# Four phase boundaries: who makes the shifted columns and one slab's low part, and where the second tile is turned

## The reference

```
for i in range(DEPTH):                                  # first block, DEPTH = 2
    mod_l = split(silu_c @ ada_w[i] + ada_b[i], 6)
    h_l = rmsnorm(x, mix_norm_g[i]) * (1 + mod_l[1]) + mod_l[0]
    y_l = mixer(h_l) if i == 0 else conformer_conv(h_l)
    x = x + mod_l[2] * y_l
    h = rmsnorm(x, ffn_norm_g[i]) * (1 + mod_l[4]) + mod_l[3]
    x = x + mod_l[5] * ((silu(h @ w1) * (h @ w3)) @ w2)
x = rmsnorm(x, final_g)
for l in range(DEPTH):                                  # second block
    x = x + 0.5 * swiglu(rms_norm(x), ffn1_w_in[l], ffn1_w_out[l])
    x = x + mixer(rms_norm(x) @ w_mix_in[l]) @ w_mix_out[l]
    x = x + 0.5 * swiglu(rms_norm(x), ffn2_w_in[l], ffn2_w_out[l])
```

## Time and profile before

| | |
|---|---|
| median of three runs | 1772.92 us |
| the profiled execution, first to last instruction (span) | 1771.1 us |
| TensorE busy | 1696.4 us (96%) |
| VectorE busy | 1104.2 us (62%) |
| ScalarE busy | 807.9 us (46%) |
| GpSimd busy | 48.2 us (3%) |
| low parts of slabs on VectorE | 258 passes, 591.2 us |
| high parts of slabs on ScalarE | 258 passes, 491.6 us |

### The profile page before, as it was taken

How to read it: one execution, slowest core, us unless ns; L and a number is a source line. 1 busy time by engine, 2 the same in 40 slices (tenths; PEclk the granted TensorE clock), 3 DMA queues, 4 the chain that set the end, 5 groups by cost and what they waited for, 6 DMA issues and landing times.

```text
span 1771.1 us, 20813 instructions
## 1 busy us (share of the span) xinstructions
PE 1696.4 (96%) x8168; PEld 1370.1 (77%) x8168; DVE 1104.2 (62%) x1284; ACT 807.9 (46%) x970; POOL 48.2 (3%) x60
## 2 busy tenths in 40 slices
PE   6999899998988999999999999999999999999999
PEld 3775678787656887788787888887888778888877
DVE  3876788877767664655547856554655458755542
ACT  3425544423445443454436555443444346664441
POOL 0001000000000000000001200000000003000000
PEclk9999999999989999999999999999999999999999
DMA  9683288887434765565555427655565454336550
GB/s 354 223 290 113 89 286 281 307 290 257 159 102 152 240 238 179 166 197 184 185 166 167 152 67 212 190 190 177 180 190 190 168 168 164 119 108 210 185 187 25
DMA packets 239985, 332.29 MB, mean 188 GB/s; under 512 B 11024, under 2 KB 191988, under 8 KB 239888
## 3 DMA queue, kind: packets, MB, share of 16 engines
q1 hardware_dynamic: 235872, 321.95, 55.0%
q10 hardware_dynamic: 2704, 5.82, 0.9%
q0 software_dynamic: 1312, 3.19, 0.7%
HBM read 329.87 MB, written 1.05 MB: 187 GB/s over the span
## 4 chain that ended last, share of the span: by engine, by line
PE 84%; DVE 9%; ACT 3%; issue 2%; DMA 1%; SPq 0%; DVEq 0%; ACTq 0%
PE bank L459 17%; PE bank L461 17%; PE bank L460 17%; PE bank L790 7%; PE bank L793 7%; PE bank L791 7%; DVE lo L1803 3%; PE bank L888 2%; DMA raw<-in_ada_w 1%; ACT hi L1285 1%; PE bank L773 1%; PE bank L1229 1%; PE bank L1230 1%; PE bank L1232 1%; PE bank L950 1%
## 5 line engine op out<-in xcount | busy, mean ns | idle before, releaser
L1803 DVE TENSOR_TENSOR lo<-raw,hi 128x2048 fp32r<-128x2048 f32 x258 | 591.2, 2295 | 382.1 <-ACT hi L1285 381.8
L1285 ACT ACTIVATE hi<-raw 128x2048 fp32r<-128x2048 f32 x258 | 491.6, 1911 | 335.5 <-PE bank L461 174.9
L459 PE MATMUL bank<-hi,XTh 128*128 128x512 f32 (+1 forms) x1424 | 564.7, 397 | 9.5 <-ACT XTh L1301 3.0
L461 PE MATMUL bank<-hi,XTl 128*128 128x512 f32 (+1 forms) x1424 | 553.3, 389 | 0.0
L460 PE MATMUL bank<-lo,XTh 128*128 128x512 f32 (+1 forms) x1424 | 552.9, 388 | 0.0
L459 PEld LDWEIGHTS bank<-hi,XTh 128*128 128x128 f32 x1424 | 268.8, 189 | 70.8 <-issue 6.2
L461 PEld LDWEIGHTS bank<-hi,XTl 128*128 128x128 f32 x1424 | 268.3, 188 | 56.0
L460 PEld LDWEIGHTS bank<-lo,XTh 128*128 128x128 f32 x1424 | 268.8, 189 | 52.7 <-issue 1.0
L790 PE MATMUL bank<-hi,HTh 128*128 128x512 f32 x528 | 208.5, 395 | 9.3 <-DVE HTl L1890 9.3
L791 PE MATMUL bank<-lo,HTh 128*128 128x512 f32 x528 | 206.6, 391 | 0.0
L793 PE MATMUL bank<-hi,HTl 128*128 128x512 f32 x528 | 164.0, 392 | 0.0
(11 more groups left out here) (363 smaller groups left out, 1412.0 us busy)
## 6 DMA issues: line engine op xcount, KB each, us to landing
raw<-in_ffn_w_in SPq DMA_DIRECT2D x176, 512.0 KB, 4.9
raw<-in_ffn_w SPq DMA_DIRECT2D x132, 512.0 KB, 4.9
raw<-in_ada_w SPq DMA_DIRECT2D x96, 512.0 KB, 5.0
raw<-in_ffn_w_out SPq DMA_DIRECT2D x88, 512.0 KB, 4.0
raw<-in_w_mix_in SPq DMA_DIRECT2D x52, 512.0 KB, 4.7
raw<-in_od_pw_w SPq DMA_DIRECT2D x24, 512.0 KB, 5.3
raw<-in_ev_w_in SPq DMA_DIRECT2D x20, 512.0 KB, 9.4
raw<-in_w_mix_out SPq DMA_DIRECT2D x16, 512.0 KB, 3.8
```

The lines of the kernel that those rows point to most:

```text
L459: pe.matmul(dst, xh, wh, start=start, stop=False)
L461: return pe.matmul(dst, xl, wh, start=False, stop=stop)
L1285: act.activation(hi[r][:, :], raw[g % RAW][:, :], ACT.Copy).then_inc(*up("hi", d))
L1803: dve.tensor_tensor(lo[r][:, :], raw[g % RAW][:, :], hi[r][:, :].bitcast(F32), ALU.subtract).then_inc(*up("lo", d))
```

## The change

It has four parts, all at boundaries 0 to 3.

1. At boundaries 0 to 2 ScalarE makes the columns of half h = 0 (four passes of 128 x 128, scale and bias read from `MODS`), VectorE those of half h = 1 alone.
2. ScalarE makes the high part of slab U+1 before it deals with the first tile's columns (at boundary 3 too).
3. The low part of slab U+3 is made by GpSimd (`lo_pool`), not by VectorE. TensorE and SyncE wait for this semaphore for these four slabs.
4. TensorE turns the second tile in the middle of slab U+3 (after two of its four blocks), not ahead of it.

```diff
--- before.py
+++ after.py
@@ -425,6 +425,12 @@
         slabs, first, dense = weight_slabs(A)
         quarter_at = {g: key[1:] for key, g in first.items() if key[0] == "ada"}
 
+        fourth = {p: first[f"up{p}"] + 3 for p in range(4)}
+
+        def low_of(d):
+
+            return "lo_pool" if d in fourth.values() else "lo"
+
         def fox_stat(i, o, n):
 
             return ST[:, 16 + 12 * i + o:16 + 12 * i + o + n]
@@ -452,7 +458,7 @@
         def tensor_engine(pe):
             def ready(d):
                 pe.wait_ge(*at("hi", d))
-                pe.wait_ge(*at("lo", d))
+                pe.wait_ge(*at(low_of(d), d))
                 return d % RING
 
             def three(dst, xh, xl, wh, wl, start, stop):
@@ -851,6 +857,9 @@
                 def products(c, half, t):
                     r = (d + 2 * c + half) % RING
                     for k in range(4):
+                        if (c, half, t, k) == (1, 1, 0, 2):
+                            turn(p, 1)
+                            after()
                         kk = 4 * half + k
                         last = three(bank[2 * c + t][:, :], XTh[:, kk, tok[t]], XTl[:, kk, tok[t]],
                                      hi[r][:, k * CH:(k + 1) * CH], lo[r][:, k * CH:(k + 1) * CH], kk == 0, kk == KD - 1)
@@ -862,9 +871,6 @@
                     for half in range(2):
                         ready(d + 2 * c + half)
                         products(c, half, 0)
-                        if (c, half) == (1, 0):
-                            turn(p, 1)
-                            after()
                 pe.wait_ge(*at("xt_hi", (p, 1, 1)))
                 pe.wait_ge(*at("xt_lo", (p, 1, 1)))
                 for c in range(2):
@@ -1500,9 +1506,18 @@
                 act.activation(st, st, ACT.Sqrt, scale=1.0 / D, bias=col("eps", 1)).then_inc(*up("std", (p, t)))
 
             def turn(p, t):
+                if p in SHIFTED:
+                    l, n = SHIFTED[p]
+                    act.wait_ge(*at("mods", ((0, 4), (1, 1, 1, "full"), (1, 4, 1, "full"))[p] if p else (0, 3, 1)))
+                    act.wait_ge(*at("turned", (p, t, 0)))
+                    for kk in range(4):
+                        last = act.activation(FULL[:, kk, tok[t]], turn_bank(p, t, 0)[:, kk * P:(kk + 1) * P], ACT.Identity,
+                                              scale=MODS[:, l, n + 1, kk:kk + 1], bias=MODS[:, l, n, kk:kk + 1])
+                    last.then_inc(*up("full_act", (p, t)))
                 for h in range(2):
                     ks = slice(4 * h, 4 * h + 4)
-                    high("xt_hi", (p, t, h), XTh[:, ks, tok[t]], FULL[:, ks, tok[t]], at("full", (p, t, h)))
+                    made = at("full_act", (p, t)) if p in SHIFTED and h == 0 else at("full", (p, t, h))
+                    high("xt_hi", (p, t, h), XTh[:, ks, tok[t]], FULL[:, ks, tok[t]], made)
 
             def down(p, late, after=None):
                 nslab, d = DOWNS[p][0], first[f"down{p}"]
@@ -1515,9 +1530,12 @@
                     if after:
                         after(s)
                 rows(p, 0)
+                if two_first(p):
+                    split(d + nslab - 3 + RING)
                 if p < 9:
                     turn(p, 0)
-                split(d + nslab - 3 + RING)
+                if not two_first(p):
+                    split(d + nslab - 3 + RING)
                 split(d + nslab - 2 + RING)
                 if two_first(p):
                     split(d + nslab - 1 + RING)
@@ -2141,8 +2159,6 @@
 
             def rows(p, t):
                 residual(p, t)
-                if t == 1 and two_first(p):
-                    split(first[f"up{p}"] - 1 + RING)
                 if p != 3 and p not in SHIFTED:
                     return
                 st = ST[:, 2 + t:3 + t] if p == 3 else ST[:, t:t + 1]
@@ -2156,7 +2172,7 @@
                     dve.tensor_scalar(XN[:, t, :], X[:, t, :], st, None, ALU.mult).then_inc(*up("normed", (p, t)))
 
             def turn(p, t):
-                for h in range(2):
+                for h in range(1 if p in SHIFTED else 0, 2):
                     b = turn_bank(p, t, h)
                     ks = slice(4 * h, 4 * h + 4)
                     dve.wait_ge(*at("turned", (p, t, h)))
@@ -2629,6 +2645,15 @@
                 ffn(3 * l + 5)
 
         def gpsimd_engine(pool):
+            def split(d):
+
+                g, r = dense[d], d % RING
+                pool.wait_ge(*at(f"landed{g % RAW}", (g, 1)))
+                pool.wait_ge(*at("used", d - RING))
+                pool.wait_ge(*at("hi", d))
+                pool.tensor_tensor(lo[r][:, :], raw[g % RAW][:, :], hi[r][:, :].bitcast(F32),
+                                   ALU.subtract).then_inc(*up("lo_pool", d))
+
             pool.memset(CS[:, :, :], 0.0).then_inc(*up("cs_zero"))
             pool.memset(ONES[:, :], 1.0).then_inc(*up("ones"))
             pool.wait_ge(*at("used", first["w_in"] + 9))
@@ -2644,6 +2669,8 @@
             pool.dma_start(TAPD[:, :, :], A["tap_turns"]).then_inc(*up("tap_in", 4, 16))
             pool.dma_start(FWD[:, :, :, :, :], A["forward"]).then_inc(*up("conv_const", 0, 16))
             pool.dma_start(INV[:, :, :], A["inverse"]).then_inc(*up("conv_const", 1, 16))
+            split(fourth[0])
+            split(fourth[1])
             pool.wait_ge(*at("added", (1, 1)))
             for h in range(2):
                 pool.dma_start(B1[:, h * D:(h + 1) * D],
@@ -2652,6 +2679,8 @@
             pool.dma_start(ZR[FREQ:FREQ + 1, :, :, :], A["conv_bias"]).then_inc(*up("conv_in", 3, 16))
             for l in range(2):
                 if l == 0:
+                    split(fourth[2])
+                    split(fourth[3])
                     pool.wait_ge(*at("rstd2", 3))
                     pool.dma_start(TRI[:, :, :], A["tri"]).then_inc(*up("consts2", 0, 16))
                     pool.dma_start(MASKF[:, :, :], A["masks"]).then_inc(*up("consts2", 1, 16))
@@ -2701,7 +2730,7 @@
                             sp.wait_ge(*at("ada_used", (l, mod, s)))
                     else:
                         sp.wait_ge(*at("hi", freed))
-                        sp.wait_ge(*at("lo", freed))
+                        sp.wait_ge(*at(low_of(freed), freed))
                 for n, (dst, src) in enumerate(parts(raw[r])):
                     sp.dma_start(dst, src).then_inc(*up(f"landed{r}", (g, n), 16))
             for t in range(T):
```

## The result

| | before | changed |
|---|---|---|
| median of 20 runs | 1772.93 us (1771.6 to 1774.78) | 1776.62 us (1774.52 to 1778.97) |
| ratio | | 1.002 (95%: 1.0013 to 1.0026) |
| profiled execution, span | 1771.1 us | 1777.1 us |

The changed kernel is slower by 3.7 us, 0.2% and clear of the interval. The forecast was 0.4 us faster. The profiled execution took 1778.45 us, near the top of its runs, and that of the second set 1776.47, its median. Where the two traces differ, the second stands nearer to the medians.

The account below looks back on a forecast made before the run. TensorE, busy 96% of the span, was taken as the bound, so only its waits count. Boundary terms -0.55, -0.1, -0.3 and +0.5 made -0.4 us: 1772.5 us from a median of 1772.92, range 1767 to 1777.5.

Parts of the forecast that it names:

- VectorE is freed earlier: Boundary 0: the 1.21 us wait goes, shared columns save 0.4; U+2's low part ends at 218.1 instead of 219.73.
- The exclusion: Boundary 0: VectorE's X+XN stands until GpSimd's instruction ends, one us later than before; XN at 225.7 instead of 225.3.
- Rivals B: Boundaries 0 to 3: GpSimd's pass runs beside VectorE's; 12.0 us gained in all, 1761; chance 0.14.
- C: Boundaries 0 to 3: GpSimd's low part goes before VectorE's low part of U+2; +5.4 us, 1778; chance 0.11.
- GpSimd's pass: Low part of U+3, boundaries 0 to 3: 4.1 us on GpSimd (3.6 or 4.8 possible), against VectorE's 2.28.
- Rival D: GpSimd's pass on a float32r output takes 6 us: 1.9 more at each boundary, +7.2, 1780; chance 0.05.
- The clock: Behind the second tile's turn: low level at boundaries 0 and 1 hidden behind the columns; at boundary 2 costs some 0.4 us.
- The sum: Boundaries 0 to 3 together: -0.55 - 0.1 - 0.3 + 0.5 = -0.4 us on a span of 1771.1.
- The turn: Second tile's turn inside U+3: gains only if XN comes before U+3 is half done; at boundary 0 TensorE waits 2.2 us.
- The pass is traded for the block: Likeliest case: VectorE's saved 2.28 us come back as GpSimd's longer pass in front of the sum; 1772.5; chance 0.66.

Follow-up runs that it names:

- the second set: The changed kernel itself, unaltered, run again on another chip (11 runs), with a second profiled execution: 1776.47 us, ratio 1.002 to the kernel before.

## Why the prediction was wrong

**VectorE is freed earlier: right.** The low part of U+2 was to end at 218.1, 12.6 us behind the first sum; it ended 12.45 behind it. ScalarE's columns were taken at 1.5 us, and took 1.51. What this gains by itself, which the prediction did not price apart, is 7.7 us.

**The exclusion: right.** Passes with two SBUF inputs stood until GpSimd's instruction ended at all four boundaries (4.32, 4.32, 4.37 for XN x GATE, 4.31). The forecast had X ready 17.7 us behind the first sum; it was ready 18.0 behind it. Rivals B (no exclusion) and C (GpSimd first) did not happen. The high part of U+3 comes at 216.5 by the prediction's own terms (213.22 + 5.50 - 1.83 - 0.4) and not at 216.7; the margin against C was real all the same, for VectorE began the low part of U+2 at 216.9 and GpSimd came at 217.75.

**GpSimd's pass: mechanism right, size off.** The term was 4.1 us; it measured 4.60 and 4.57. The four-fold 512 columns were too low: the nearest rows have single columns, repeated, as one input, and the pass here reads two full tiles (512 columns of those took some 1.25 us in the run with four pieces). The bound of 4.8 us (eight times the 256-column pass) was nearer. The Trainium skill's GPSIMD Engine Reference, "Elementwise — side-by-side cycle accounting", which gives 4497 ns for it, is 0.1 us short of this trace and was nearer than my value. Set against the sum: the second tile was to start 0.55, 0.1 and 0.6 us earlier at boundaries 0 to 2 and 0.5 later at 3, 0.75 earlier in all; it started 0.56 later, and 1.06 in the second execution. This step is 1.3 us of the 4.1 that the forecast missed (1.8 in the second execution, where the turn of boundary 2 was at the low clock). Rival D, 6 us, is what the recorded 5.89 seems to say; but 1.3 of it is waiting for VectorE.

**The clock: this step failed.** The prediction took the start of the second tile's products as its quantity, since "behind it nothing is changed". It placed the low level right behind the turn and let "those six slow products" be "hidden behind the columns", with 0.4 us at boundary 2. The low level came later, in the second tile's products, in six of eight passages through a boundary in two executions, where nothing hides it. In the first execution that took 5.3 us by U+4 (1.3 to 1.8 at each of the first three boundaries), in the second 1.9. What went ahead of it at boundary 0: TensorE stood for 0.48, 1.88 and 1.91 us within 8.4 us, with six products and the turn between, where before it stood once ahead of the turn, for 1.93 us, and not at all ahead of the second tile's products. I looked at the busy gap before the turn, and not at the second gap that the moved turn puts in front of the second tile.

That it is the moved turn is seen when all traces are put side by side, by the granted clock in the first 4 us of the second tile's products. In the five kernels that turn ahead of U+3 (one of them with filler products) it is 1.00 in 20 of 20 passages. In the six traces with the turn in mid slab and no filler it is 0.69 or less in 12 of 24, and 1.00 in the others: 4 and 2 of 4 in the two executions of the changed kernel, 3 with the turn alone, 1 with the low part back on VectorE, 2 with GpSimd writing only, none with the four pieces. Why a passage with the same waits goes one way or the other stays open.

What this step is worth in the medians isn't settled. The turn alone lost 5.6 us, in its trace mostly this way; the fillers give back 0 to 2 us and cost something themselves.

**The sum.** From the first sum of boundary 0 to the end of the span the changed kernel loses 4.8 us in the first execution and 2.2 in the second. With the forecast's gain of 0.4 that makes a miss of 5.2 and 2.6, and the medians' 4.1 (2.7 to 5.0 by the interval of the ratio) lies between. How much of it is the pass and how much the clock differs from execution to execution, as the start of the second tile (+0.56, +1.06 us) and what follows it (5.3, 1.9) show.

**The turn: its rule was wrong.** The prediction said that moving the turn buys something only if XN comes before U+3 is half done. The runs point the other way. Where XN is late, TensorE fills its wait with half a slab, and the second tile starts 0.7 to 1.7 us sooner. Where XN is early, the turn has to wait for the half slab: at boundary 0 the second tile starts 23.05 us behind the first sum with the turn in mid slab and 22.42 with the turn ahead, since the columns take 4.3 to 4.4 us from the turn either way. Nothing is gained then. The 5.6 us that it costs alone are, by its trace, for the most part the clock's.

**The balance.** "The pass is traded for the block" is right as a mechanism and hides what mattered: the two sides are -8 and +11 us, not small numbers. A forecast near zero from two such terms hangs on the size of each. The chance of 0.59 for no difference, with 1776.5 as its upper end, had its place for an error in GpSimd's pass (up to +2.2 us) and none for a low clock behind the second tile's start.

## What to carry to other kernels

Before work is moved to an idle GpSimd, look at which of VectorE's passes with two SBUF inputs will be asked for while it runs: the price is not GpSimd's time but how late the last of these comes, and cutting the pass into pieces gave back 5.8 of 11 us here, some of it by the clock. When a wait is moved to just ahead of a stretch of dense products, look at the granted clock in those products too, and at more than one execution. Try the parts of a change apart: here two of four gained 0.5%, and the other two lost that and 0.2% more.

## What the runs showed of the hardware

- GpSimd's pass over 128 x 2048, two inputs, float32r out, takes 4.57 to 4.60 us; cut into four, 216.50 to 223.77 with VectorE's low part (until 217.80) and its sum of 1.23 us in it, some 1.25 us for each piece. Fills of the same size take 1.82 us and neither stop VectorE's two-input passes nor are stopped.
- VectorE's scaling of XN, with one tile of SBUF as input, is stopped too: 1.18 us at 223.15, against 0.75 in the changed kernel and 0.76 before, while GpSimd's last piece ran until 223.77. The Trainium skill's SBUF — State Buffer, "Who interferes with whom", counts `tensor_scalar` among the passes that can take the shared ports by their mode; the trace agrees, with the 0.43 us more.
- ScalarE's four 128 x 128 passes with scale and bias from tiles take 1.51 us, not much more than VectorE's four (1.37 us).
- What a stretch at the low clock costs depends on what stands behind it: 0.4 us at boundary 0 before, where a wait for the columns would have taken up the rest, and 1.3 to 1.8 us in the second tile's products, which have no slack. In those products the clock was low in none of 20 passages with the turn ahead of U+3, and in 12 of 24 with the turn in mid slab and no filler.
- The same kernel can lose to the low clock in different places: at boundary 0 the changed kernel's was low in one execution (0.64 between 232 and 236 us) and not in the other (1.00), with the same waits of 1.9 us ahead.
